# Scores on the compressed keys: one fp32 product per head, or two accumulating fp32r products on keys in two parts

## What is computed

```
k_cmp = compress(kc, cmp_pos[0], cmp_w1[0], cmp_w2[0])
...
s_c = jnp.einsum('bqgrd,bngd->bgrqn', qblk, k_cmp).astype(f32) * scale
p_c = masked_softmax(s_c, cmp_end[None, :] <= tpos[:, None])
o_cmp = jnp.einsum('bgrqn,bngd->bqgrd', p_c, v_cmp32)
```

## Time and profile before

| | us |
|---|---|
| Median of 3 runs | 1487.67 |
| Lowest and highest of them | 1487.56, 1491.05 |
| Span of the profiled execution, first to last instruction | 1488.8 |
| Time of that execution beyond the span | not given separately |
| TensorE matmuls busy | 1434.8 (96%) |
| TensorE weight loads busy | 1184.6 (80%) |
| VectorE, ScalarE, GpSimd busy | 618.9, 512.3, 649.0 |

### The profile page before, as it was taken

How to read it: one execution, slowest core, us unless ns; L and a number is a source line. 1 busy time by engine, 2 the same in 40 slices (tenths; PEclk the granted TensorE clock), 3 DMA queues, 4 the chain that set the end, 5 groups by cost and what they waited for, 6 DMA issues and landing times.

```text
span 1488.8 us, 17728 instructions
## 1 busy us (share of the span) xinstructions
PE 1434.8 (96%) x7179; PEld 1184.6 (80%) x7179; DVE 618.9 (42%) x1047; ACT 512.3 (34%) x679; POOL 649.0 (44%) x298
## 2 busy tenths in 40 slices
PE   5799999989999999999999999999999999999998
PEld 4688887877788888888877888787778888888886
DVE  5726356758454444442220562674514112121131
ACT  4322444552333333321132142535524333332111
POOL 0434225233454455444643423343164545454552
PEclk8899999999999999999999999999999999999999
DMA  9632110044266665654332321100032333232331
GB/s 366 193 94 93 57 57 29 1 142 170 73 181 184 189 193 171 195 192 162 130 114 60 114 86 57 58 1 1 24 91 82 88 95 104 85 113 78 103 103 57
DMA packets 181973, 163.19 MB, mean 110 GB/s; under 512 B 16037, under 2 KB 147589, under 8 KB 181893
## 3 DMA queue, kind: packets, MB, share of 16 engines
q1 hardware_dynamic: 180724, 161.83, 34.4%
q10 hardware_dynamic: 1169, 0.25, 0.1%
HBM read 159.96 MB, written 2.10 MB: 109 GB/s over the span
## 4 chain that ended last, share of the span: by engine, by line
PE 81%; issue 6%; DVE 4%; ACT 3%; POOL 3%; POOLq 2%; DMA 1%; DVEq 0%; ACTq 0%; SPq 0%
PE psum L1547 19%; PE psum L1549 18%; PE psum L1548 18%; PE psum L1579 4%; PE psum L1580 4%; PE psum L1582 3%; PE psum L1866 2%; POOL w_lo L560 2%; ACT w_hi L727 1%; PE psum L1588 1%; PE psum L1710 1%; PE psum L1731 1%; PE psum L1513 1%; DVE psum L1068 1%; PE psum L1527 1%
## 5 line engine op out<-in xcount | busy, mean ns | idle before, releaser
L560 POOL TENSOR_TENSOR w_lo<-w_raw,w_hi 128x2048 fp32r<-128x2048 f32 x76 | 350.8, 4616 | 474.0 <-ACT w_hi L727 473.1
L727 ACT ACTIVATE w_hi<-w_raw 128x2048 fp32r<-128x2048 f32 (+2 forms) x104 | 192.9, 1854 | 620.2 <-PE psum L1549 484.4
L1547 PE MATMUL psum<-h_hi,w_hi 128*128 128x512 f32 x928 | 367.0, 395 | 3.2 <-POOL w_lo L560 2.2
L1549 PE MATMUL psum<-h_hi,w_lo 128*128 128x512 f32 x928 | 361.5, 390 | 0.0
L1548 PE MATMUL psum<-h_lo,w_hi 128*128 128x512 f32 x928 | 361.3, 389 | 0.0
L1547 PEld LDWEIGHTS psum<-h_hi,w_hi 128*128 128x128 f32 x928 | 174.4, 188 | 39.5 <-POOL w_lo L560 3.1
L1549 PEld LDWEIGHTS psum<-h_hi,w_lo 128*128 128x128 f32 x928 | 174.2, 188 | 37.1
L1548 PEld LDWEIGHTS psum<-h_lo,w_hi 128*128 128x128 f32 x928 | 174.4, 188 | 34.7
L565 POOL TENSOR_TENSOR w_lo<-w_raw,w_hi 128x1792 fp32r<-128x1792 f32 (+2 forms) x28 | 112.4, 4013 | 144.7 <-ACT w_hi L727 144.7
L1447 DVE SCALAR_TENSOR_TENSOR fy<-psum,par,fy 128x511 f32<-128x511 f32 x44 | 33.0, 750 | 277.9 <-ACT fy L927 277.9
L1547 PE MATMUL psum<-hid_hi,w_hi 128*128 128x512 f32 x352 | 137.9, 392 | 0.0
(11 more groups left out here) (266 smaller groups left out, 1913.3 us busy)
## 6 DMA issues: line engine op xcount, KB each, us to landing
w_raw<-in_ffn_up SPq DMA_DIRECT2D x88, 512.0 KB, 4.9
a_raw<-in_ada_w SPq DMA_DIRECT2D x56, 512.0 KB, 4.6
w_raw<-in_w_in SPq DMA_DIRECT2D x48, 512.0 KB, 4.4
w_raw<-in_ffn_down SPq DMA_DIRECT2D x32, 512.0 KB, 4.4
w_raw<-in_w_out SPq DMA_DIRECT2D x16, 512.0 KB, 4.3
a_raw<-in_ada_w SPq DMA_DIRECT2D x6, 1024.0 KB, 6.7
a_tok<-in_ada_w SPq DMA_DIRECT2D x6, 1024.0 KB, 7.3
w_raw<-in_ffn_down SPq DMA_DIRECT2D x16, 384.0 KB, 3.0
```

The source lines that it names most:

```text
L560: g.tensor_tensor(w_lo[:, slot_of(l, u), :], w_raw[:, slot_of(l, u), :], w_hi[:, u % HI, :].bitcast(F32), ALU.subtract).then_inc(s_lo, 1)
L727: s.activation(w_hi[:, u % HI, 0:n], w_raw[:, r, 0:n], ACT.Copy).then_inc(s_hi, 1)
L1547: m(ps, l_hi, r_hi, start=first, stop=False)
L1549: return m(ps, l_lo, r_hi, start=False, stop=last)
```

## The change

`kcmp` holds the keys in two fp32r parts in place of one fp32 tile. The copy out of bank 5 writes the first part, rounded to fp32r; after a drain a subtraction writes the rest as the second part. Each head's scores become two products on fp32r operands that accumulate in the same 32 columns, with the same 128 query columns as weights. The products' place in the order, the semaphores and everything behind the scores stay.

```diff
-        kcmp = att.place("kcmp", [P, NG, NCP])
+        kcmp = att.place("kcmp", [P, 2, NG * NCP], F32R)
...
-                v.tensor_copy(kcmp[:].rearrange("p g n -> p (g n)"), bank[5][:, 0:NG * NCP])
+                v.tensor_copy(kcmp[:, 0, :], bank[5][:, 0:NG * NCP])
+                dve.drain()
+                v.tensor_tensor(kcmp[:, 1, :], bank[5][:, 0:NG * NCP], kcmp[:, 0, :].bitcast(F32), ALU.subtract)
...
                     for h in range(NH):
-                        last = m(bank[4 + t][:, h * NCP:(h + 1) * NCP], qk[:, h, t * P:(t + 1) * P].bitcast(F32),
-                                 kcmp[:, h // R, :], start=True, stop=True)
+                        for part in range(2):
+                            last = m(bank[4 + t][:, h * NCP:(h + 1) * NCP], qk[:, h, t * P:(t + 1) * P],
+                                     kcmp[:, part, h // R * NCP:(h // R + 1) * NCP], start=part == 0, stop=part == 1)
```

## The result

| | before | after |
|---|---|---|
| Median, us | 1488.08 | 1496.86 |
| Lowest, highest of 8 runs, us | 1487.06, 1491.05 | 1488.61, 1497.86 |
| Ratio after to before, 95% interval | | 1.0038 [1.0023, 1.0053] |
| Span of the profiled execution, us | 1488.8 | 1486.8 |

The change makes the kernel slower, by about 0.4%: the ratio goes nearly with the means, 1488.57 and 1494.46 us, while the medians lie 0.6% apart. The spread of the changed kernel is the first thing to read: its profiled execution is the fastest of the 8 and is shorter than that of the kernel before, so a comparison of these two profiles alone would give the wrong sign.

A forecast was written before the change was run, and what follows sets the result against it. TensorE was taken to bound the kernel, weight loads setting the scores' pace. Matmuls 0 plus DVE 0.60 us on the 1487.67 us median gave 1488.3 us, range 1484.5 to 1492.0.

The forecast's parts named there:

- The product count: Scores on TensorE: 64 fp32 products become 128 fp32r products, still 128 load and matmul pairs, 0 us.
- the load-bound pace: Scores blocks on TensorE: weight loads set 106 ns per product, columns are free, a block of 16 stays 1.70 us.
- the subtraction: Added on DVE behind the kcmp copy and a drain: 128x64 with one PSUM operand, 224 ns.
- the shift of the vcmp copy: On DVE, the first vcmp copy starts about 0.43 us after the kcmp copy in place of 0.13.
- the longer wait: TensorE's idle time before the first scores block grows by 0.3 us per layer, to about 1.05 us.
- A: Scores weight loads get cheap, or one load serves both parts of a head: 1481.5 us, faster by 0.4%; chance 0.06.
- B: In the scores, a narrow fp32r product is slower than a load: at 150 ns each, 1493.9 us; chance 0.04.
- D: In the scores, fp32r operands still run as two passes, 256 pairs: +13.6 us, 1502 us; chance 0.01.
- rival C: Halved streamed columns make TensorE's clock fall in the scores: up to +10 us, 1498 us; chance 0.03.
- The clock over the scores stretch still 1.00: Sign for the profile after: TensorE's granted clock stays at full speed through the scores, as before.
- the DVE part: Drain and subtraction ahead of the vcmp copies delay TensorE uncovered: 0.30 us x 2 layers = +0.60 us.
- what a fall costs: One TensorE clock fall costs at most 1.5 us; in the scores, three or more decide the sign.

The follow-up runs named there:

- k_early: Changed kernel with TensorE released by the subtraction, before the vcmp copies, for which the second scores block waits; median 1486.71 us, 0.9989 of the kernel before.
- c_dve_only: Kernel before, plus the drain and a subtraction into an unread tile ahead of the vcmp copies, scores still fp32; median 1497.17 us, ratio 1.0055.
- d_mm_only: Changed kernel without the drain and subtraction, both products reading the first, rounded part of the keys; median 1499.24 us, 1.0058 of the kernel before.
- b_wide: Changed kernel with each scores product moving both groups' keys, 64 columns in place of 32; median 1495.49 us, 1.0036 of the kernel before.
- i_dve_behind: Kernel before, plus a drain and a subtraction into an unread tile on VectorE, behind the last vcmp copy and TensorE's release; median 1490.50 us, ratio 1.0008.
- e_one_load: Changed kernel with one 64-column fp32r product per head moving both key parts, VectorE adding the halves; median 1484.15 us, 0.9973 of the kernel before.
- h_wide_fill: Changed kernel with 64-column scores products and three unused 512-column bf16 products in front of the wait; median 1489.56 us, 1.0007 of the kernel before.
- g_fill: Changed kernel plus three unused 512-column bf16 products in front of the wait for the keys; median 1489.50 us, 1.0013 of the kernel before.

## Why the prediction was wrong

**Right: the instructions.** The product count, the load-bound pace (1.71 us for a block at full clock, forecast 1.70), the subtraction (225 ns, forecast 224), the shift of the vcmp copy (0.43 us) and the longer wait (+0.30 us per layer) all came as worked out. Rivals A, B and D are out: 128 pairs, 1.71 us for a block, and loads of fp32r that keep fp32's duration (191 ns both, in k_early and the earlier trace rows). The fast load that the Trainium skill gives to other types than FP32 (TensorE: Matmul & The Clock Gate, section Weight-path perf modes) did not come. The delay of 0.60 us in all is seen in the traces alone; the falls hide it in the times. One reading of the prediction was off without effect on the sum: L1731 is printed in the earlier trace rows, with 1% of the chain.

**Wrong: the step that set the clock aside.** The prediction said of rival C: "Against: the clock now is 1.00 there, and between two blocks stand six 512-column products", and gave it 0.03. Full clock in one execution says that the clock held there once; it does not say by how much it was clear of a fall. The sign "The clock over the scores stretch still 1.00" failed in the very first profile after (0.51 from 188.7 to 192.1). The runs showed that the margin was very small: 0.30 us more wait in each layer, with nothing else changed on TensorE (c_dve_only), put 11 of 11 runs over 1494 us, and the matmul part at the old wait (d_mm_only) 9 of 12. Rival C named the right event, but tied it to the halved columns alone; c_dve_only has all its columns and falls, and b_wide got them back and still falls.

**Wrong: the term of the DVE part.** "The cover is nothing: 0.30 us x 2 layers = +0.60 us" counted the wait by its length only. In the stretch where it stands it also brings long falls of the clock. c_dve_only measures the term at 1497.17 us against 1490.80 in the same series, 6.4 us in the medians, some ten times the 0.60. i_dve_behind, the same kind of work without the wait, has no run at 1494 us and no clear difference from the kernel before (1.0008 [0.9997, 1.0019]).

**Wrong: what a fall costs.** The prediction priced a fall at 1.5 us, as a single one, and let three of them decide the sign. In the stretch of the scores a fall is long: 13.7 us at 0.50 in c_dve_only and b_wide, 20.5 us in d_mm_only, and 6.3 us are lost within the stretch in c_dve_only. One of them decides.

**What stays open.** That thin work is what the clock answers to is the reading that fits all thirteen kernels; no run shows the mechanism itself. That the slow runs of the changed kernel have the long falls of b, c and d is inferred from their times and clocks. The kernels with falls and those that took them away ran in different series; only the kernel before ran in all. Why the falls come in some runs and not in others was not settled; that they differ in place and number between runs of one kernel is what was seen. The two terms were varied in steps, so the runs give no border between dense enough and too thin, and 64 columns at the long wait (7 of 12) against 32 (13 of 19 over both series) is no clear difference. In d_mm_only the products changed in columns and in type together; no run had fp32r products of 64 columns at the old wait, so that the columns are its cause is an inference, for which e_one_load (fp32r, no fall) and, weakly, h_wide_fill against g_fill speak.

## What to carry to other kernels

Where small products bound by weight loads stand between large ones, look at TensorE's clock as a resource with a margin: 0.3 us more wait in each layer, 0.6 us on paper, cost some 6 us here. Releasing TensorE earlier or halving the loads took all of it back, and filling the wait with spare products most of it. Moving both parts of a split operand in one product (64 columns under one load) was worth more than the choice of type. And time such a change in ten or more runs with the mean clock beside each; the one profile taken of it may show the lucky case.

## What the runs showed of the hardware

The pace of the weight loads follows the granted clock: a block of 16 loads with 32 columns took 1.70 us at 1.00 and 3.27 us at 0.50 (c_dve_only, layer 1). Narrow fp32r products came 107 ns apart with 32 columns (1.71 us for 16) and 101 ns apart with 64 (0.81 us for 8), so 32 more columns cost nothing. In d_mm_only TensorE's clock fell although the matmul records were busy for 36.7 of the 37.1 us in front of it and the longest idle time was 0.77 us by the load queue, and it stayed down for 20.5 us with the matmul records busy in all of them.
